# A two-layer block on one core: channel order in the second projection, gate rows through DRAM, and conditioning tiles dealt over both MLPs

## The reference

```python
mod = (silu(c) @ w_ada + b_ada)              # 6 x 2048: sh1, sc1, g1, sh2, sc2, g2
h = x * (1 + sc1) + sh1
z = h @ w_in + b_in
z_u, z_v, z_h, z_g = split(z, [1024, 2048, 5120])
y_a = spatial_gating(gelu(z_u), gelu(z_v), ...) @ w_branch_a   # layer norm of v over channels, 128x128 mixing
y_b = hyena(z_h, ...) @ w_branch_b           # 3-tap conv of 3 x 1024 channels, then two gated long convolutions
gate_a, gate_b = split(sigmoid(z_g), 2)
mix = (gate_a * y_a + gate_b * y_b) @ w_o + b_o
x = layer_norm(alpha * x + g1 * mix)
h = x * (1 + sc2) + sh2
f = square(relu(h @ w_m1 + b_m1)) @ w_m2 + b_m2
x = layer_norm(alpha * x + g2 * f)
```

## Time and profile before

| | |
|---|---|
| median of three runs | 2507.66 us (2507.03 to 2510.01) |
| profiled execution, its time | 2509.39 us |
| its span, first to last instruction | 2507.6 us |
| busy: PE, DVE, ACT, POOL | 97%, 69%, 41%, 1% |
| mean granted clock of TensorE | 0.990 |
| DMA | 553.33 MB, mean 221 GB/s |

### The profile page before, as it was taken

How to read it: one execution, slowest core, us unless ns; L and a number is a source line. 1 busy time by engine, 2 the same in 40 slices (tenths; PEclk the granted TensorE clock), 3 DMA queues, 4 the chain that set the end, 5 groups by cost and what they waited for, 6 DMA issues and landing times.

```text
span 2507.6 us, 31135 instructions
## 1 busy us (share of the span) xinstructions
PE 2430.1 (97%) x13494; PEld 2079.7 (83%) x13494; DVE 1735.3 (69%) x1629; ACT 1033.1 (41%) x947; POOL 22.0 (1%) x46
## 2 busy tenths in 40 slices
PE   7999999999999999989999999999899999999998
PEld 7898888778778878778888888998788888888886
DVE  7776577877677777766778777667775555655655
ACT  4453454334334334354544334343543343343442
POOL 0000000000000000000000000000000000000000
PEclk9999999999999999999999999999999999999999
DMA  7333467777786787866776444645545555555552
GB/s 265 130 120 133 160 227 269 282 293 266 274 316 263 297 328 276 316 268 220 282 283 248 158 180 185 237 168 199 188 183 190 192 189 189 188 193 187 187 197 101
DMA packets 78728, 553.33 MB, mean 221 GB/s; under 512 B 8794, under 2 KB 10997, under 8 KB 12672
## 3 DMA queue, kind: packets, MB, share of 16 engines
q1 hardware_dynamic: 74832, 528.25, 56.5%
q0 software_dynamic: 3760, 23.10, 2.5%
HBM read 542.92 MB, written 8.39 MB: 220 GB/s over the span
## 4 chain that ended last, share of the span: by engine, by line
PE 84%; DVE 8%; DMA 4%; ACT 3%; issue 1%; SPq 0%; ACTq 0%; DVEq 0%
PE ps L545 25%; PE ps L546 13%; PE ps L558 10%; PE ps L560 10%; PE ps L559 10%; DMA stage<-wstream 4%; DVE w_lo L1365 3%; ACT w_hi L974 2%; PE ps L513 2%; PE ps L543 2%; PE ps L514 2%; PE ps L515 2%; PE ps L542 1%; PE ps L899 1%; PE ps L571 1%
## 5 line engine op out<-in xcount | busy, mean ns | idle before, releaser
L1365 DVE TENSOR_TENSOR w_lo<-stage,w_hi 128x2048 fp32r<-128x2048 f32 x402 | 918.0, 2288 | 474.7 <-ACT w_hi L974 472.2
L974 ACT ACTIVATE w_hi<-stage 128x2048 fp32r<-128x2048 f32 x402 | 766.3, 1911 | 818.8 <-DMA stage<-wstream 356.2
L545 PE MATMUL ps<-xs,w_hi 128*128 128x512 f32 x3000 | 1066.2, 399 | 9.2 <-DVE w_lo L1365 7.2
L546 PE MATMUL ps<-xs,w_lo 128*128 128x256 f32 x3000 | 842.0, 281 | 0.0
L545 PEld LDWEIGHTS ps<-xs,w_hi 128*128 128x128 f32 x3000 | 563.9, 188 | 147.0 <-DVE w_lo L1365 9.7
L546 PEld LDWEIGHTS ps<-xs,w_lo 128*128 128x128 f32 x3000 | 567.2, 189 | 4.9 <-issue 1.2
L558 PE MATMUL ps<-w_hi,hs 128*128 128x512 f32 x1024 | 402.8, 393 | 17.8 <-DVE w_lo L1365 17.8
L559 PE MATMUL ps<-w_hi,hs 128*128 128x512 f32 x1024 | 399.8, 390 | 0.0
L560 PE MATMUL ps<-w_lo,hs 128*128 128x512 f32 x1024 | 399.6, 390 | 0.0
L558 PEld LDWEIGHTS ps<-w_hi,hs 128*128 128x128 f32 x1024 | 192.9, 188 | 64.8 <-DVE w_lo L1365 23.1
L1667 DVE SCALAR_TENSOR_TENSOR stage<-stage,cond 128x2048 f32<-128x2048 f32 x96 | 219.4, 2286 | 24.3 <-DMA stage<-wstream 24.3
(11 more groups left out here) (381 smaller groups left out, 2394.4 us busy)
## 6 DMA issues: line engine op xcount, KB each, us to landing
stage<-wstream SPq DMA_DIRECT2D x497, 1024.0 KB, 4.8
spectra<-k_made POOLq DMA_DIRECT2D x4, 1024.0 KB, 9.4
k_spec<-spectra POOLq DMA_DIRECT2D x4, 1024.0 KB, 5.6
xraw<-xT SPq DMA_DIRECT2D x4, 512.0 KB, 11.1
resid<-x SPq DMA_DIRECT2D x2, 1024.0 KB, 15.3
parked<-resid POOLq DMA_DIRECT2D x1, 2048.0 KB, 7.5
resid<-parked POOLq DMA_DIRECT2D x1, 2048.0 KB, 8.2
out<-out_t SPq DMA_DIRECT2D x4, 512.0 KB, 2.6
```

The costliest lines, as they stand in the source:

```text
L545: pe.matmul(o2, hi, rhs[:, k, :], start=(first and j == 0), stop=False)
L546: mm = pe.matmul(o2[:, S:2 * S], lo, rhs[:, k, 0:S], start=False, stop=False)
L974: act.activation(w_hi[:, w % HIGH, 0:m], stage[:, n % RING, 0:m], ACT.Copy).then_inc(hi_ready, 1)
L1365: tt(w_lo[:, slot, 0:m], stage[:, slot, 0:m], f(w_hi[:, w % HIGH, 0:m]), ALU.subtract).then_inc(lo_ready, 1)
```

## The change

- The columns of the z stage come as v, u, convolution, gate_b, gate_a. So the convolution's input is there sixteen tiles earlier; the tables of its steps move, and the four parts lie ten tiles apart. gate_b, u, v and the transposed v change places in memory; the first write of gate_b waits until branch A's input is made.
- For a convolution unit ACT adds the bias in its copy and does the middle tap (`middle_tap`); DVE does the two side taps one step later (`side_taps`).
- The channel sums: DVE folds eight blocks into one by three additions (`fold_sums`), and PE does one matmul for each sum, behind Z+10 and Z+14. The scale by gain and shift goes from DVE to ACT (step Z+17); the transposes go to Z+18 and Z+20, the mixing to Z+22.
- The gates' columns go to DRAM as 2048 separate numbers each (`gates`), and come back as rows for all 128 partitions. `spread`, `rows` and the two row copies fall away.
- Conditioning tiles: 68 in the first MLP (15, 16, 17 and 20 in its quarters, each evenly, the last over 28 tiles), 12 in the z stage (two in three from Z+3 to Z+19), 16 in the second MLP (one in two from the middle of its second quarter). For these `cond` is stored to DRAM before the first MLP and loaded again in the second.
- In the second MLP the results of three quarters are summed in `f_sum`; the product with g2 is taken once, in the last quarter.

```diff
-TURN_AT = {37: 0, 47: 1, 57: 2, 62: 3}
+TURN_AT = {26: 0, 36: 1, 46: 2, 56: 3}
...
-PARTS_AT = {46: 0, 56: 1, 63: 2, 70: 3}
-BACK_AT = {46: 0, 57: 1, 64: 2, 71: 3}
...
-GATE_AT = {50: 0, 59: 1, 66: 2, 73: 3}
+PARTS_AT = {34: 0, 44: 1, 54: 2, 64: 3}
+BACK_AT = {36: 0, 46: 1, 56: 2, 66: 3}
...
+GATE_AT = {38: 0, 48: 1, 58: 2, 68: 3}
+DEALT = (0, 15, 31, 48, 68)
 def stream_order():
-    for step in range(T_MLP1, T_BA):
+    for step in range(T_MLP1, N_TILES - 2):
         order.append(("w", step + 2))
-        q, l = divmod(step - T_MLP1, QT)
-        if step >= T_Z:
-            due = 78 + min(18, max(0, step - T_Z - 3) * 9 // 16)
-        elif l < UPT:
-            due = 20 * q + (9 if q == 3 else 8) * (l + 1) // 16
-        elif q == 3:
-            due = 69 + min(9, 9 * (l - UPT + 1) // 11)
+        if step < T_Z:
+            q, l = divmod(step - T_MLP1, QT)
+            of = DEALT[q + 1] - DEALT[q]
+            due = DEALT[q] + min(of, of * (l + 1) // (28 if q == 3 else 32))
+        elif step < T_MLP2:
+            due = DEALT[4] + min(12, max(0, step - T_Z - 1) * 2 // 3)
         else:
-            due = 20 * q + 8 + 12 * (l - UPT + 1) // 16
+            due = 80 + min(16, max(0, step - T_MLP2 - QT - UPT) // 2)
 # POOL
         pool.wait_ge(sem("cond_made"), 1)
+        pool.dma_start(cond_kept, cond[:]).then_inc(sem("cond_moved"), 16)
         pool.dma_start(feats[:], dram["feats"]).then_inc(sem("hid_loaded"), 16)
...
+        pool.wait_ge(sem("gate_columns"), 1)
+        pool.dma_start(gates[0].rearrange("c p -> p c"), mod[:, 32:48], allow_slow_non_contiguous=True).then_inc(sem("gate_stored"), 16)
         pool.wait_ge(tile_done, T_Z)
...
         pool.wait_ge(sem("yb_split"), 2)
+        pool.wait_ge(sem("gate_stored"), 16)
+        pool.dma_start(g1_row[:], gates[0:1].rearrange("a c p -> a (c p)").broadcast_to([P, D])).then_inc(
+            sem("gate_loaded"), 16)
...
+        pool.dma_start(cond_2[:], cond_kept).then_inc(sem("cond_moved"), 16)
+        pool.wait_ge(sem("gate_columns"), 2)
+        pool.dma_start(gates[1].rearrange("c p -> p c"), mod[:, 80:96], allow_slow_non_contiguous=True).then_inc(sem("gate_stored"), 16)
+        pool.wait_ge(sem("gate_stored"), 32)
+        pool.dma_start(g2_row[:], gates[1:2].rearrange("a c p -> a (c p)").broadcast_to([P, D])).then_inc(
+            sem("gate_loaded"), 16)
 # PE, z stage
-            if w == T_Z + 9:
-                pe.wait_ge(evac_done, U_Z + 4)
-                stats(z_v, SGUC, True, True).then_inc(sem("v_meaned"), 1)
-            if w == T_Z + 13:
-                for g in range(2):
-                    pe.wait_ge(sem("v_squared"), g + 1)
-                    stats(sq[:, g], 4, g == 0, g == 1, bank=5).then_inc(sem("v_summed"), 1)
+            if w in (T_Z + 10, T_Z + 14):
+                j = (w - T_Z - 10) // 4
+                pe.wait_ge(sem("v_folded"), j + 1)
+                stats(sq[:, 1], 1, True, True, bank=4 + j).then_inc(sem("v_summed"), 1)
 # PE, branch B
-            if w == T_BB + 4:
-                pe.wait_ge(sem("g1_diags"), 1)
-                rows().then_inc(sem("g1_spread"), 1)
 # ACT, z stage
+        def middle_tap(u):
+            act.wait_ge(psum_free[u % 2], u // 2 + 1)
+            for c in range(2):
+                k = 2 * (u - U_Z - 8) + c
+                ins = act.activation(z_h[:, k, :], tev[:, u % 2, c], ACT.Identity, bias=col("conv_b", k),
+                                     scale=col("conv_w", HYC + k))
+            ins.then_inc(sem("middle_done"), 1)
...
+            if w == T_Z + 17:
+                act.wait_ge(sem("v_centered"), 2)
+                for g in range(SGUC):
+                    ins = act.activation(z_v[:, g, :], z_v[:, g, :], ACT.Identity, bias=col("sgu_b", g),
+                                         scale=col("sgu_g", g))
+                ins.then_inc(sem("v_normed"), 1)
 # DVE, z stage
+        def fold_sums(src):
+            link(tt(sq[:, 1], src[:, 0:4], src[:, 4:8], ALU.add))
+            link(tt(sq[:, 1, 0:2], sq[:, 1, 0:2], sq[:, 1, 2:4], ALU.add))
+            tt(sq[:, 1, 0], sq[:, 1, 0], sq[:, 1, 1], ALU.add).then_inc(sem("v_folded"), 1)
 # DVE, second MLP
+                if q:
+                    condition(w + 2, cond_2)
...
+            if q == 3 and l == 0:
+                dve.wait_ge(ada_mac, N_ADA)
+                tt(mod[:, 80:96], mod[:, 80:96], col("b_ada", 80, DC), ALU.add).then_inc(sem("gate_columns"), 1)
+            if q == 3 and l in (10, 12):
+                t = l // 2 - 5
+                dve.wait_ge(sem("gate_loaded"), 32)
+                link(tt(f_sum[:, t, :], f_sum[:, t, :], g2_row[:], ALU.mult))
+            if q == 3 and l in (14, 16):
+                t = l // 2 - 7
+                link(tt(resid[:, t, :], resid[:, t, :], f_sum[:, t, :], ALU.add))
...
                     if q == 0:
-                        ins = tt(step_t[:, t], o2, bm_row[:, b], ALU.add)
+                        ins = tt(f_sum[:, t, b], o2, bm_row[:, b], ALU.add)
+                    elif q < 3:
+                        ins = tt(f_sum[:, t, b], o2, f_sum[:, t, b], ALU.add)
                     else:
                         ins = tt(step_t[:, t], o2, g2_row[:, b], ALU.mult)
 # host: column order of w_in
-    order = np.r_[D // 2:D, 0:D // 2, gates + D:gates + 2 * D, D:gates, gates:gates + D]
+    order = np.r_[D // 2:D, 0:D // 2, D:gates, gates + D:gates + 2 * D, gates:gates + D]
```

More of the change, by code:

```diff
@@ L102, in stream_order @@
     assert a == N_ADA
-    return order + [("w", w) for w in range(T_BA + 2, N_TILES)]
+    return order
 ORDER = stream_order()
@@ L625, in turn_block @@
                                       resid[:, t, a:a + P], ident[:])
[L626 to L632, removed]
             return mm
@@ L1265, in _ @@
                 before = job(w - 1)[1]
-                if not U_Z + 16 <= before < U_Z + 28:
+                if U_Z + 8 <= before < U_Z + 20:
+                    middle_tap(before)
+                else:
                     take_z(before)
@@ L1279, in _ @@
                 act.wait_ge(evac_done, u - 1)
[L1280 to L1284 removed]
+                if 8 <= i < 20:
+                    for c in range(2):
+                        ins = act.activation(tev[:, u % 2, c], ps[:, b + c, S:2 * S], ACT.Identity,
+                                             bias=col("b_in", 2 * i + c))
+                    ins.then_inc(cross_ready, 1)
+                else:
+                    act.activation(tev[:, u % 2], ps[:, b:b + 2, S:2 * S], ACT.Copy).then_inc(cross_ready, 1)
+            if w == T_Z + 15:
+                root()
+            if w == T_Z + 17:
[4 more added lines that the diff above has]
+                ins.then_inc(sem("v_normed"), 1)
+            if w in (T_Z + 18, T_Z + 20):
+                j = (w - T_Z - 18) // 2
                 act.wait_ge(sem("vn_turned"), j + 1)
@@ L1688, in _ @@
             split(w + 2)
-            condition(w + 2)
+            condition(w + 2, cond)
             if w == T_MLP1:
@@ L1850, in conv_work, with side_taps @@
                 gate(GATE_AT[a])
+        def fold_sums(src):
+            link(tt(sq[:, 1], src[:, 0:4], src[:, 4:8], ALU.add))
+            link(tt(sq[:, 1, 0:2], sq[:, 1, 0:2], sq[:, 1, 2:4], ALU.add))
+            tt(sq[:, 1, 0], sq[:, 1, 0], sq[:, 1, 1], ALU.add).then_inc(sem("v_folded"), 1)
+        def side_taps(u):
+            dve.wait_ge(sem("middle_done"), u - U_Z - 7)
+            t = tev[:, u % 2]
+            for c in range(2):
+                k = 2 * (u - U_Z - 8) + c
+                link(stt(z_h[:, k, 1:S], t[:, c, 0:S - 1], col("conv_w", k), z_h[:, k, 1:S], ALU.mult, ALU.add))
+                ins = stt(z_h[:, k, 0:S - 1], t[:, c, 1:S], col("conv_w", 2 * HYC + k), z_h[:, k, 0:S - 1], ALU.mult,
+                          ALU.add)
+            ins.then_inc(evac_done, 1)
         for w in range(T_Z, T_BA):
             split(w + 2)
-            condition(w + 2)
+            condition(w + 2, cond)
+            if w > T_Z and ends(w - 1) and U_Z + 8 <= job(w - 1)[1] < U_Z + 20:
+                side_taps(job(w - 1)[1])
             _, u, _ = job(w)
@@ L1875, in _ @@
-            conv_work(w - T_Z)
+                took(tt(t, acc(u), t, ALU.add), u)
+            conv_work(w - T_Z)
+            if w == T_Z + 9:
+                dve.wait_ge(evac_done, U_Z + 4)
+                fold_sums(z_v)
+            if w == T_Z + 13:
+                dve.wait_ge(sem("v_squared"), 1)
+                fold_sums(sq[:].rearrange("p g c s -> p (g c) s"))
             if w == T_Z + 11:
-                dve.wait_ge(evac_done, U_Z + 4)
-                dve.wait_ge(sem("v_meaned"), 1)
+                dve.wait_ge(sem("v_summed"), 1)
@@ L1879, in _ @@
                 link(ts(va[:], ps[:, 4, 0:S], 1.0 / 1024, None, ALU.mult))
                 tt(z_v[:], z_v[:], over(va, SGUC), ALU.subtract).then_inc(sem("v_centered"), 1)
-            if w == T_Z + 14:
+            if w == T_Z + 15:
                 dve.wait_ge(sem("v_summed"), 2)
```

(4 more changed lines are left out.)

135 lines of the change are left out of this document (55 added, 80 removed).

## The result

The changed kernel takes 2490.42 us (median of four runs, 2489.88 to 2493.11) against 2508.28 us for the kernel before (four runs, 2507.03 to 2510.01): a ratio of 0.9931, 95% interval 0.9918 to 0.9944. It is faster, but by 18 us and not by the 47.5 forecast; 2490 lies outside the range of 2450 to 2482. The profiled execution took 2493.11 us, its span 2491.3.

A forecast was written before the change was run, and what follows sets the result against it. PE, busy 97% of the span, was taken to bound the kernel through its own work and its waits. Gains of 51.8 us less 4.3 lost, net 47.5, gave 2460 us, range 2450 to 2482.

The forecast's parts named there:

- branch stage: Window from 1666.43: row spread and row copy leave the ACT and DVE loop per tile, 2.9 us gained.
- wait for v_normed: Window from 1216.60: PE's wait at the transposes goes with the normalization step on ACT and transposes two tiles later, 2.3 us.
- transform back: Convolution's transform back, window from 1397.66: PE's wait goes as the convolution's parts lie ten tiles apart, 5.8 us gained.
- spectrum stores: Three first-MLP windows where 1 MB filter-spectrum stores delay ring loads: even dealing regains 17.7 us, less a 0.8 remnant.
- third quarter, start of the fourth: First MLP, windows from 832.50 and 923.29: losses at three-in-four dealing go, 3.7 and 2.0 us.
- filter window: Window from 421.67, DVE late with filter work: dealt tiles fall two tiles later, 3 of 3.7 us gained.
- last quarter: First MLP's last quarter: 20 conditioning tiles in 28 lose 3.6 us (0 to 6.5) in place of 5.1, gaining 1.5.
- first gate store: End of the first MLP: its competition with ring loads costs nothing to 6.2 us, taken as 1.
- DVE before the sums: z-stage tiles 9 to 16: 49 us of DVE work in 46, costing 0 to 3 us, taken as 1.
- third rival: Second gate row comes late at tile 10 of the last quarter, stopping PE; about 2530 us at 60 ns a number; chance 0.05.
- second rival: DVE becomes the bound at z tiles 9 to 16 and in the first MLP's last quarter: 7 more, 2467 us; chance 0.10.
- first rival: First MLP's losses stay because the store alone, not the dealing, delays the ring: 17.7 us back, 2478 us; chance 0.15.

The follow-up runs named there:

- e2: Changed kernel with the two channel-sum matmuls one tile later, behind z tiles 11 and 15: 2483.28 us, ratio 0.9901.
- e8: Changed kernel with the first gate store's 8 KB written at the same place as 128 rows of 64 B: 2477.46 us, ratio 0.9877.
- e4: Changed kernel with conditioning tiles dealt 18, 18, 18 and 14 in the first MLP's quarters: 2482.21 us, ratio 0.9901.
- e5: Changed kernel with the earlier dealing (8 in 16, 12 in 16) in the first MLP's first three quarters, 8 in 28 in the last: 2498.79 us, ratio 0.9963.
- e13: Changed kernel with gate store in the z stage, sums, transposes and mix one tile later, conditioning dealt 15, 16, 17, 17, then 15: 2460.85 us, ratio 0.9801.
- e6: Kernel before the change with only the first gate store of 2048 numbers added, read by nothing: 2510.77 us, ratio 1.0014.
- e1: Changed kernel with the first gate store issued behind the second spectrum load of the z stage: 2476.32 us, ratio 0.9873.

## Why the prediction was wrong

The mechanisms on the gaining side held, and so did most of their sizes; the branch stage gave 0.5 of 2.9 us, and the wait for v_normed 1.3 of 2.3:

| term | counted | measured |
|---|---|---|
| row spreads, sums' matmuls | 7.1 + 5.8 | about as counted: 11.52 in place of 15.08; 39.84 for seven tiles and two sums (e2) |
| transform back | 5.8 | 5.8: 15.73 is two tiles and 40 passes |
| spectrum stores | 17.7 - 0.8 | 17.4 |
| third quarter, start of the fourth | 5.7 | 5.7 |
| filter window | 3 | 2.2: 23.52 in place of 25.69 |
| wait for v_normed | 2.3 | 1.3: of 18.80 us, 16.95 are tiles and 0.9 transposes |
| branch stage | 2.9 | 0.5 |
| last quarter | +1.5 | -3.4 (8.5 lost, 5.1 before) |
| first gate store | -1 | -14.4 |
| DVE before the sums | -1 | -11.4 |
| dealing in the z stage | -1.5 | in the row above |
| net | 47.5 | 16.6 (the spans: 16.3) |

Three terms of the sum were mis-sized, and each was a cost "taken as 1" or as the middle of its bounds.

*The gate store's competition with ring loads*, 1 us with a bound of 6.2 from "the worst spectrum store's". The bound was from the wrong row: it took a store of 1 MB to be worse than one of 8 KB, a price by bytes. The price of the earlier trace rows, at most 25 ns a number, was used only for how long the store itself takes; there it was far too high (16.9 us for 2048 numbers). What it does to the other queue was not asked. Two windows of the changed kernel's DMA queue of ring loads, 10 us each, first 1040 to 1050 us, then 1072 to 1082 (packets, MB, share of 16 engines):

```profile
q1 hardware_dynamic: 362, 2.57, 68.6%
```

```profile
q1 hardware_dynamic: 66, 0.41, 85.0%
q0 software_dynamic: 17, 0.00, 0.2%
```

In the second window, most of it between the start of the store's packets and its landing (1083.0), the ring gets a sixth of its bytes, and the engines count as busier than before: of the 160 us that 16 engines have in 10 us, a ring packet takes 0.85 x 160 / 66 = 2.1 us on average, in place of 0.686 x 160 / 362 = 0.30. The store itself (q0) hardly shows. The profile lists it as 32 packets of 256 B, 64 numbers each, all begun from 1071.05 to 1072.06, and 16 of 4 B behind them. By what way it slows the ring's packets the trace does not show. The Trainium skill's page DMA: Bandwidth & Descriptors, section Rules for kernel authors, says to rearrange a strided last dimension, since it becomes one descriptor for each element. e8 agrees with the advice: the same bytes in rows of 64 B landed after 5.8 us and cost nothing. The number of descriptors stands in no trace. The third rival drew only the store's own lateness from this, and there the second gate store (15.3 us, no wait on PE) shows that nothing was at risk.

*DVE before the sums*, 1 us with bounds of 0 and 3 from a balance of work, 49 us in 46. The balance was not what decides: DVE was busy 39.82 of 51.25 us. What decides is order. The fold stands behind a split, which waits for ACT's w_hi and the ring, and behind a conditioning pass, so it ended half a tile after PE had asked for it, twice 3.2 us. The other 5 us are matmuls at a lower clock behind these waits, which the bound left out: PE was busy 44.92 us in place of e2's 39.84 for 230 matmuls each (mean clock 0.90 in that window).

*The last quarter's rate*, 3.6 us between 0 and 6.5; 8.5 were lost. The upper bound was drawn from tok tiles, and 79.04 - 73.46 = 5.6 of the 8.5 us are lost in up tiles. DVE and ACT of the changed kernel, where tiles 148 to 150 are split:

```profile
959.01 2.28 DVE L1687 SCALAR_TENSOR_TENSOR stage<-stage,cond 128x2048 f32<-128x2048 f32 x1
961.22 2.28 DVE L1385 TENSOR_TENSOR w_lo<-stage,w_hi 128x2048 fp32r<-128x2048 f32 x1
963.42 2.28 DVE L1687 SCALAR_TENSOR_TENSOR stage<-stage,cond 128x2048 f32<-128x2048 f32 x1
```

```profile
967.08 0.63 ACT L1194 ACTIVATE hs<-tev 128x512 fp32r<-128x512 f32 x1 [6.26 <-DVE tev L1702]
967.62 1.90 ACT L976 ACTIVATE w_hi<-stage 128x2048 fp32r<-128x2048 f32 x1
```

Two conditioning passes in neighbouring steps make DVE's take of an up unit late; ACT waits for it (6.26 us), and its next split stands behind that wait, and behind the split PE (1.2 us at tile 150). At 14 in 28 (e4) ACT's wait there is 4.3 us, and PE's waits for w_lo at up tiles are down from 2.6 us in sum to 0.5.

The second rival named both of these places, but as DVE at its limit and at 7 us together. The first rival is out (e5). The slower side never came near: everything that had been forecast to gain did so, at least in part. With the three losses taken away (e13) the kernel takes 2460.85 us, near the 2460 forecast, but by way of remedies that the forecast did not name. That it comes so near is in part luck: the branch stage gave 2.4 us less than counted, and the remedies took away costs that the forecast had left in. Why the branch stage gave 0.5 in place of 2.9 (two waits of PE, 1.0 and 0.7 us, stay) is left open.

## What to carry to other kernels

Bound what a new transfer does to the others by its form, how many pieces and how small, and not by its bytes alone, and put it where the stream that it may stop has tiles to spare. The load to look at is the first one that will not have landed by then: here one issued 0.6 us ahead of the store was caught, while ones issued some 2 us ahead landed in time. Where an engine works down a list, a balance of busy time does not bound how late a result comes: write down what stands ahead of the new instruction in its step, and what that waits for. When a wait is priced, the matmuls at the lower clock behind it belong to the price.

## What the runs showed that was not expected

- A store of 2048 numbers of 4 B from 128 partitions to DRAM landed after 13.5 to 16.9 us in these runs, half of it after 13.1, and 128 rows of 64 B, the same 8 KB, after 5.8. During the first a 1 MB load took 17.7 us in place of 4.9, and the DMA's busy share (85%) hid it: 41 GB/s moved.
- The same store cost 14.4, 10.4 (21.24 - 10.88, e4), 7.1 (e5), 2.9 (e6) and 0 us (e1), by how far ahead of need the loads were that it caught. In the first three the load of tile 168 was caught, and the load ahead of it had landed 4.7, 8.8 and 11.4 us before its tile began.
